# A hybrid mixer network on one core: score blocks, gate products and normaliser sums issued over two and four column groups

## The chip, the cores and the metric

The kernel runs on one core of one Trainium2 chip. The metric is the device time of one execution in microseconds (us), the median of several runs. TensorE (PE in the profile, PEld for its weight loads), VectorE (DVE), ScalarE (ACT), GpSimd (POOL) and the DMA queues run beside each other and meet at semaphores. Everything is float32; each product in the source becomes two matmul instructions with a weight load each.

## The reference

Two streams of 128 tokens (prompt and sample), width 1024, go through four layers. A layer is a mixer and a mixture of 16 experts; the mixers are attention, mLSTM, gated linear attention (GLA), attention. What the change touches:

```
# mLSTM, 8 heads: gates from 32 columns of the input projection
g = (p[..., 2*qk_w + 2*v_w:] + b_gates).reshape(B, T, 2, 2, H)   # direction, gate, head
# state for the last token: the normaliser, per direction and head
n_new = decay * n + einsum('bsh,bshd->bhd', ws, kc)
# GLA: scores inside a chunk, 4 heads x 2 streams, two directions
A = einsum('bcthd,bcshd,bctshd->bchts', qc, kc, exp(diff))       # s <= t
```

The 256 tokens of both streams lie on the free axis of most products, so a product has 256 columns.

## The kernel before, in words

Every engine has its own program, written out by hand; the order of work on an engine is the order of its lines. Weights come in chunks of 2 MB over SyncE's queue (`load`, L462 to L468), in the order of a list (`plan_chunks`, L120). Six ring slots hold them, and three more places in the expert stages. The load of a chunk into a slot waits until TensorE has used the chunk that was there before (`used`, L402); so loads are paced by TensorE's progress.

**mLSTM gates.** POOL fetches the 32 gate columns in four pieces at the start (L532) into `WGT`, which holds for each of 8 slices k of the width two blocks of 40 columns (input gates, forget gates; direction 0 in columns 0 to 7, direction 1 in 32 to 39). TensorE's `mlstm` (L1162 to L1169) multiplies slice by slice: for the first gate, k = 0 to 7 as the slices of the normalised input `H` become ready (`h_ready`, L1025: ScalarE's L618 and VectorE's L1716 write them), then k = 0 to 7 for the second gate. Both go into bank 7 of PSUM. VectorE adds the biases and takes an absolute value (L1794 to L1796, semaphore step `l_abs`). TensorE waits for `l_abs` before the first group of the input projection (L1175), since bank 7 is used later in that stage for modulation rows. ScalarE waits for the same step, applies Exp and Ln (L685, L686), and then copies the projection results out (L695); VectorE continues with scans and the short convolution (L1798 to L1827).

**Input projection.** 16 groups of 8 products (`group`, L962, matmuls at L966), 4 from each chunk, then the rows of two modulation chunks (`mod_rows`, L990 to L997). In `mod_rows` the 8 slices go to four column groups of the array: slice k writes partitions 32*(k%4) to 32*(k%4)+31 of bank 7 with 32-column weights.

**Normaliser.** Within the output projection of mLSTM (L1333 to L1335) eight products, one for each head, add into one result of 8 partitions. The weights of head h are 8 columns cut from a constant with a single column of ones, so that head h lands in row h. ScalarE copies the 8 rows (L809) and stores them with one DMA (L810). Before the next norm ScalarE waits for all small stores (L947).

**GLA.** In `gla` the eight groups i of the gate projection (L1396) alternate with eight blocks of scores (L1399 to L1406). Block i has the 32 query rows of block `blk` of direction d as weights (32 columns) and the keys of one of two buffers `gKI[:, i % 2]` as moving data (128 columns), 8 products for heads and streams. It writes partitions 32*blk to 32*blk+31 of two banks. Before it TensorE waits until the keys are written (`g_ki`, VectorE L1956); VectorE waits for `g_a` before it writes a key buffer again (L1952) and clears both between the directions (L1954). `turn_keys` (L1376) and `state` (L1384) lie between later blocks. ScalarE applies the exponentials of the keys (L847) and copies the groups (L849).

**Expert stages.** Each layer ends with a stage of 8 pairs of experts (L1538, L1549 and others), 96 MB of weights.

Of the kernel before, what the change touches and what calls it, by code (L numbers as in the profile page):

```python
# [17 lines left out]
ALU = mybir.AluOpType  # L18
ACT = mybir.ActivationFunctionType
AX = mybir.AxisListType  # L20

P = 128
# [21 lines left out]
def constants():  # L44
# [35 lines left out]
    add("fold", (i[:, None] % 32 == np.arange(32)[None, :]))  # L80
    add("first", np.broadcast_to(np.tril(np.ones((4, 4)), -1).reshape(1, 16), (P, 16)))
# [69 lines left out]
def plan_slots():  # L151
# [25 lines left out]
    "tensor_step": ["prmT", "a_rotk0", "a_dup0", "l_g", "l_at", "l_kt", "l_n",  # L177
# [3 lines left out]
    "scalar_step": ["cs", "l_rowexp", "l_n_sb", "g_u_sb", "g_se", "g_gate", "g_root0", "g_root1", "y_sq0", "y_sq1", "y_sq2", "y_sq3", "y_root"],  # L181
# [20 lines left out]
def program(nc, I, O):  # L202

    with ExitStack() as ctx:
# [25 lines left out]
        WGT = sb("WGT", [P, KD, 2, 40])  # L230
# [110 lines left out]
        mJ = WGT[:, :, :, :].rearrange("p a b c -> p (a b c)")[:, 0:256]  # L341
# [20 lines left out]
        WA1 = WGT[:, :, :, :].rearrange("p a b c -> p (a b c)")[:, 0:512].rearrange("p (k n) -> p k n", k=KD)  # L362
# [98 lines left out]
        def _(sp):  # L461
# [54 lines left out]
            sp.wait_ge(S("out"), 16 * (4 + 3 + 2 + 2))  # L516
# [7 lines left out]
        def _(pool):  # L524
# [3 lines left out]
            gates = I["mlstm1_w_in"].rearrange("(k p) n -> p k n", p=P)[:, :, 6144:6176]  # L528
            for d in range(2):
                for g in range(2):  # L530
                    at = 16 * d + 8 * g
                    pool.dma_start(WGT[:, :, g, 32 * d:32 * d + 8], gates[:, :, at:at + 8]).then_inc(S("load_g"), 16)  # L532
                    pool.dma_start(BGT[32 * d:32 * d + 8, g:g + 1],
                                   I["mlstm1_b_gates"][at:at + 8].rearrange("(h o) -> h o", o=1)).then_inc(S("load_g"), 16)
                pool.dma_start(M0[32 * d:32 * d + 8, 1:2], I["state_mlstm_m_1"][0, d].rearrange("(h o) -> h o", o=1)).then_inc(S("load_g"), 16)
# [13 lines left out]
            pool.wait_ge(S("out"), 80)  # L549
# [6 lines left out]
            pool.wait_ge(S("out"), 80)  # L556
# [9 lines left out]
        def _(act):  # L566
# [115 lines left out]
            def mlstm():  # L682
                E = mROW[0:40, 2]
                after(act, "l_abs")
# [124 lines left out]
                run(A(mJ[0:8], PS[0:8, 4, 0:N2], ACT.Copy), "l_n_sb")  # L809
                load(O["n"][0].rearrange("d h k -> h d k"), mJ[0:8].rearrange("h (d k) -> h d k", d=2), "out")  # L810
# [129 lines left out]
            for l in range(DEPTH):  # L940
                norm(2 * l)
                if l == 0:
                    mods(0)
                affine(2 * l, l, 0)
                wait(act, "back", 32 * l)
                (lambda: attention(l // 3, l), mlstm, gla)[l % 3]()
                act.wait_ge(S("out"), (32, 80, 112, 144)[l])  # L947
                norm(2 * l + 1)
                affine(2 * l + 1, l, 3)
                moe(l)  # L950
# [8 lines left out]
        def _(pe):  # L959
# [202 lines left out]
            def mlstm():  # L1162
                pe.wait_ge(S("load_g"), 16 * 11)
                for g in range(2):
                    for k in range(KD):
                        if g == 0:
                            h_ready(2, k)
                        ins = mm(PS[0:40, 7, N2 * g:N2 * g + N2], WGT[:, k, g], H[:, k], start=(k == 0), stop=(k == KD - 1))
                ins.then_inc(S("l_g"), 1)  # L1169
                for c in range(4):  # L1170
                    w = landed(pe, POS["min", 1, c])
                    for m in range(4 * c, 4 * c + 4):
                        wait(pe, "l_raw", m - 3)
                        if m == 0:
                            after(pe, "l_abs")  # L1175
                        group(bank(m % 4, 0, N2), zip(tile(w, m % 4), [H[:, k] for k in range(KD)]), "l_qk")
                    mod_run(2, 2 * c, 2 * c + 2)
# [131 lines left out]
                for c in range(2):  # L1309
                    for r in range(2):  # L1310
                        w = landed(pe, POS["mout", 1, (c, r)])
                        for m in range(4):
# [18 lines left out]
                            if c == 1 and r == 1 and m == 0:  # L1331
                                pe.wait_ge(S("l_c_sb"), 5)
                                for h in range(MH):  # L1333
                                    ins = mm(PS[0:8, 4, 0:N2], c_("win")[:, 40 - h:48 - h], mKW[:, h].rearrange("p a b -> p (a b)"), start=(h == 0), stop=(h == MH - 1))
                                ins.then_inc(S("l_n"), 1)  # L1335

            def gla():
# [54 lines left out]
                for i in range(2 * NB):  # L1392
# [81 lines left out]
            def moe(l):  # L1474
                n0 = POS["wg", l, 0]
                n = 2 * l + 1
                if l == 0:
                    pe.wait_ge(S("load_g"), 16 * 11)
# [192 lines left out]
        def _(v):  # L1671
# [117 lines left out]
            def mlstm():  # L1789
# [3 lines left out]
                v.wait_ge(S("load_g"), 16 * 11)  # L1793
                run(ts(gi, PS[0:40, 7, 0:N2], BGT[:, 0:1], None, ALU.add), "dve")  # L1794
                run(ts(gf, PS[0:40, 7, N2:512], BGT[:, 1:2], None, ALU.add), "dve")
# [420 lines left out]
```

## Time and profile before

| | |
|---|---|
| median of 3 runs | 1841.28 us (1840.45 to 1841.54) |
| span of the profiled execution | 1840.1 us |
| own time of the profiled execution | not listed; the median stands 1.2 us above the span |
| TensorE busy | 1752.0 us, 95% |
| DMA read | 606.67 MB, 335 GB/s over the span |
| mLSTM mixer with its gates | about 427 to 764 us |
| GLA mixer | about 1018 to 1191 us |

In the rows a line begins with its start in us and its length. "PE L966 MATMUL ... x64" is a run of 64 matmul instructions of line 966 of the kernel. "[1.68 <-DVE ...]" says that the engine had been idle for 1.68 us, and what ended it.

### The profile page before, as it was taken

To read this page: it belongs to the slowest core of one execution; us is meant where nothing else is said; L and a number is where in the kernel's file an instruction comes from. 1 tells how busy PE (TensorE), PEld (TensorE's weight loads), DVE (VectorE), ACT (ScalarE), POOL (GpSimd) and SP (SyncE) were. 2 spreads that over 40 slices of the span, in tenths; PEclk is the share of its full clock that TensorE was granted. 3 is DMA by queue.
4 is the path that set the end of the run, shared out by engine and by line. 5 is a ranking of instruction groups with operands and counts; after the bars stand their busy time and mean duration, and the time that the engine had idled before them with its cause. 6 is when DMAs were issued, how large, how long until landed. Compare 5 with 4: busy or idle time off the path is not lost.

```text
span 1840.1 us, 21589 instructions
## 1 busy us (share of the span) xinstructions
PE 1752.0 (95%) x8789; PEld 1023.2 (56%) x8789; DVE 475.1 (26%) x1237; ACT 378.3 (21%) x761; POOL 40.6 (2%) x52
## 2 busy tenths in 40 slices
PE   5899999999998979999998999999999999999996
PEld 3578544446744868844444747854444687544433
DVE  2142411115300261321111254251111252511112
ACT  2232200003102480300001233220000342200001
POOL 1000000000000000000000000000000000000000
PEclk9999899999999999999999999999999999899999
DMA  9988699998999235489999795869999819699993
GB/s 343 382 292 372 259 425 425 427 420 293 355 366 316 95 134 206 152 327 427 427 427 410 280 358 207 325 260 420 427 428 421 312 67 387 242 423 426 427 427 145
DMA packets 134526, 609.99 MB, mean 332 GB/s; under 512 B 12485, under 2 KB 19269, under 8 KB 109592
## 3 DMA queue, kind: packets, MB, share of 16 engines
q1 hardware_dynamic: 117408, 589.84, 80.5%
q10 hardware_dynamic: 12504, 10.70, 1.9%
q0 software_dynamic: 4512, 8.02, 1.2%
q8 instruction: 73, 1.20, 0.3%
q14 instruction: 29, 0.24, 0.0%
HBM read 606.67 MB, written 8.92 MB: 335 GB/s over the span
## 4 chain that ended last, share of the span: by engine, by line
PE 82%; DMA 9%; DVE 4%; ACT 2%; issue 1%; SPq 1%; ACTq 0%; DVEq 0%; POOLq 0%
PE PS L966 22%; PE PS L1538 21%; PE PS L1549 11%; PE PS L1502 7%; PE PS L996 4%; DMA ring<-in_moe_wg 3%; PE PS L1049 3%; DMA arena<-in_moe_wu 2%; DMA arena<-token_rows,IDX 2%; DVE arena L2095 1%; DMA ring<-in_attn_w_qkv 1%; PE PS L1017 1%; PE PS L1482 1%; DMA ring<-in_w_mod 1%; PE PS L1543 1%
## 5 line engine op out<-in xcount | busy, mean ns | idle before, releaser
L1538 PE MATMUL PS<-ring,arena 128*64 128x512 f32 x1280 | 375.4, 601 | 4.4 <-DMA ring<-in_moe_wg 4.0
L900 ACT ACTIVATE arena<-PS 128x512 f32<-128x512 f32 (+1 forms) x130 | 70.6, 543 | 803.5 <-PE PS L1529 351.8
L1538 PEld LDWEIGHTS PS<-ring,arena 128*64 128x64 f32 x1280 | 117.0, 138 | 181.6 <-issue 181.6
L2095 DVE TENSOR_TENSOR arena<-arena,PS 128x512 f32<-128x512 f32 x32 | 33.5, 1047 | 641.7 <-PE PS L1538 641.7
L966 PE MATMUL PS<-HS,ring 128*128 128x256 f32 x768 | 175.1, 386 | 4.6 <-ACT arena L735 2.9
L1538 PE MATMUL PS<-arena 128*64 128x512 f32 x576 | 169.6, 594 | 0.0
L966 PEld LDWEIGHTS PS<-HS,ring 128*128 128x128 f32 x768 | 146.0, 193 | 31.0 <-issue 8.3
L966 PE MATMUL PS<-arena,ring 128*128 128x256 f32 x640 | 143.6, 384 | 8.3 <-DVE arena L1893 6.2
L1502 PE MATMUL PS<-arena 128*128 128x256 f32 (+3 forms) x688 | 144.6, 361 | 6.1 <-ACT arena L900 3.7
L1549 PE MATMUL PS<-ring,arena 128*64 128x512 f32 x640 | 141.7, 595 | 0.0
L1502 PEld LDWEIGHTS PS<-arena 128*128 128x128 f32 (+1 forms) x688 | 112.2, 190 | 45.1 <-issue 22.7
L966 PEld LDWEIGHTS PS<-arena,ring 128*128 128x128 f32 x640 | 122.6, 193 | 26.4 <-issue 8.1
L966 PE MATMUL PS<-ring,HS 128*128 128x512 f32 (+1 forms) x256 | 105.0, 568 | 0.0
L1538 PE MATMUL PS<-HS,arena 128*64 128x512 f32 x192 | 92.9, 641 | 0.0
L996 PE MATMUL PS<-ring,CS 128*32 128x512 f32 x768 | 89.8, 606 | 1.9 <-issue 1.3
L1549 PEld LDWEIGHTS PS<-ring,arena 128*64 128x64 f32 x640 | 44.1, 137 | 83.3 <-issue 80.5
L1549 PE MATMUL PS<-arena 128*64 128x512 f32 x192 | 84.9, 595 | 0.1
L1549 PE MATMUL PS<-HS,arena 128*64 128x512 f32 x192 | 85.0, 595 | 0.0
L2076 DVE COPY arena<-PS 128x512 f32<-128x512 f32 (+1 forms) x100 | 68.6, 686 | 52.6 <-PE PS L1543 26.2
L1538 PEld LDWEIGHTS PS<-arena 128*64 128x64 f32 x576 | 52.5, 137 | 53.2 <-issue 53.2
L966 PEld LDWEIGHTS PS<-ring,HS 128*128 128x128 f32 x256 | 48.1, 190 | 56.1 <-issue 55.2
L1049 PE MATMUL PS<-HS,ring 128*128 128x256 f32 x256 | 63.0, 392 | 3.8 <-DMA ring<-in_attn_w_qkv 3.8
(344 smaller groups left out, 1631.9 us busy)
## 6 DMA issues: line engine op xcount, KB each, us to landing
ring<-in_w_mod SPq DMA_DIRECT2D x48, 2048.0 KB, 16.4
ring<-in_moe_wu SPq DMA_DIRECT2D x41, 2048.0 KB, 20.5
ring<-in_moe_wd SPq DMA_DIRECT2D x41, 2048.0 KB, 21.7
ring<-in_moe_wg SPq DMA_DIRECT2D x41, 2048.0 KB, 20.4
arena<-in_moe_wg SPq DMA_DIRECT2D x24, 2048.0 KB, 18.1
HS<-in_moe_wu SPq DMA_DIRECT2D x12, 2048.0 KB, 18.6
arena<-in_moe_wu SPq DMA_DIRECT2D x12, 2048.0 KB, 21.2
arena<-in_moe_wd SPq DMA_DIRECT2D x12, 2048.0 KB, 25.9
```

Source lines behind the costliest of these rows:

```text
L900: A(dst, src, func).then_inc(S(sem), 1)
L966: ins = mm(out, a, b, start=first and i == 0, stop=final and i == len(pairs) - 1)
L996: ins = mm(PS[r:r + 32, 7, :], CS[:, k, 30 - 2 * i:62 - 2 * i], w[:, k], start=(i == 0 and k < 4), stop=(i == len(MODS[g]) - 1 and k >= 4))
L1017: ins = mm(bank(7 if n else 5, 0, N2), ones, SQ[:, k], start=(k == 0), stop=(k == KD - 1))
L1049: ins = mm(bank(5 + m % 2, 0, N2), w[:, k, P * (m % 4):P * (m % 4) + P], H[:, k], start=(k == 0), stop=(k == KD - 1))
L1482: ins = mm(bank(4 + s, 0, NE), H[:, k, T * s:T * s + T], RW[:, k], start=(k == 0), stop=(k == KD - 1))
L1502: return mm(out, rows, onehot, start=first, stop=final, skip_group_check=True)
L1538: ins = mm(PS[64 * e:64 * e + 64, b, :], XG[:, k, 64 * e:64 * e + 64], w[:, k], start=(k == 0), stop=(k == KD - 1))
L1543: ins = tp(bank(b, P * f, P * f + P), HID[:, P * f:P * f + P], ident)
L1549: ins = mm(PS[64 * e:64 * e + 64, b, :], HTS[:, f, 64 * e:64 * e + 64], w[:, f, 512 * j:512 * j + 512], start=(f == 0), stop=(f == 3))
L2076: v.tensor_copy(dst, src).then_inc(S(sem), 1)
L2095: tt(by_k(HID), row(SG), row(bank(here[1])), ALU.mult).then_inc(S("hid"), 1)
```

## The change

It alters three places.

1. **Gates.** `WGT` gets 512 columns; one DMA brings all 32 gate columns, so that slice k has one 32-column weight. Eight products (slice k to column group k%4, bank 6) take the place of sixteen. ScalarE copies bank 6 to `mGP`. Two more products with a constant of 0 and 1 (`foldg`) add the four partial sums and spread them to the 40 rows that VectorE expects, in bank 5. These stand behind group m = 0 of the input projection, and the wait for `l_abs` moves from before group 0 to behind group 3.
2. **Normaliser.** Head h goes to column group h%4, with 32-column weights; heads h and h+4 share a group. ScalarE copies all 128 partitions, and four DMAs of two rows each take the place of one. The counts of the waits for stores follow.
3. **GLA scores.** Blocks i-1 and i are issued together behind group i for odd i, product by product in turn; they write different partitions. `turn_keys(0)` moves from behind block 2 to behind blocks 2 and 3.

```diff
@@ constants
+    foldg = np.zeros((P, 2, 40))
+    for g in range(2):
+        for d in range(2):
+            for h in range(MH):
+                foldg[:, g, 32 * d + h] = (i % 32 == 16 * d + 8 * g + h)
+    add("foldg", foldg.reshape(P, 80))
@@ gpsimd
+            pool.dma_start(mWG, gates).then_inc(S("load_g"), 16)
...
-                    pool.dma_start(WGT[:, :, g, 32 * d:32 * d + 8], gates[:, :, at:at + 8]).then_inc(S("load_g"), 16)
@@ scalar, mlstm
+                after(act, "l_gp")
+                run(A(mGP, bank(6, 0, N2), ACT.Copy), "l_gp_sb")
                 after(act, "l_abs")
...
-                run(A(mJ[0:8], PS[0:8, 4, 0:N2], ACT.Copy), "l_n_sb")
-                load(O["n"][0].rearrange("d h k -> h d k"), mJ[0:8].rearrange("h (d k) -> h d k", d=2), "out")
+                run(A(mJ, bank(4, 0, N2), ACT.Copy), "l_n_sb")
+                for j in range(4):
+                    load(O["n"][0].rearrange("d (r j) k -> j r d k", j=4)[j], mJ[32 * j:32 * j + 2].rearrange("r (d k) -> r d k", d=2), "out")
...
-                act.wait_ge(S("out"), (32, 80, 112, 144)[l])
+                act.wait_ge(S("out"), (32, 128, 160, 192)[l])
@@ tensor, mlstm
-                for g in range(2):
-                    for k in range(KD):
-                        if g == 0:
-                            h_ready(2, k)
-                        ins = mm(PS[0:40, 7, N2 * g:N2 * g + N2], WGT[:, k, g], H[:, k], start=(k == 0), stop=(k == KD - 1))
-                ins.then_inc(S("l_g"), 1)
+                for k in range(KD):
+                    h_ready(2, k)
+                    r = 32 * (k % 4)
+                    ins = mm(PS[r:r + 32, 6, 0:N2], mWG[:, k], H[:, k], start=(k < 4), stop=(k >= 4))
+                ins.then_inc(S("l_gp"), 1)
+
+                def gates():
+
+                    after(pe, "l_gp_sb")
+                    for g in range(2):
+                        ins = mm(PS[0:40, 5, N2 * g:N2 * g + N2], c_("foldg")[:, 40 * g:40 * g + 40], mGP, start=True, stop=True)
+                    ins.then_inc(S("l_g"), 1)
+
...
                         wait(pe, "l_raw", m - 3)
+                        group(bank(m % 4, 0, N2), zip(tile(w, m % 4), [H[:, k] for k in range(KD)]), "l_qk")
                         if m == 0:
+                            gates()
+                        if m == 3:
                             after(pe, "l_abs")
-                        group(bank(m % 4, 0, N2), zip(tile(w, m % 4), [H[:, k] for k in range(KD)]), "l_qk")
...
-                                    ins = mm(PS[0:8, 4, 0:N2], c_("win")[:, 40 - h:48 - h], mKW[:, h].rearrange("p a b -> p (a b)"), start=(h == 0), stop=(h == MH - 1))
+                                    ins = mm(PS[32 * (h % 4):32 * (h % 4) + 32, 4, 0:N2], c_("win")[:, 40 - h // 4:72 - h // 4], mKW[:, h].rearrange("p a b -> p (a b)"), start=(h < 4), stop=(h >= 4))
@@ tensor, gla
-                    d, blk, lo, hi = gla_block(i)
-                    pe.wait_ge(S("g_v_sb"), 4)
-                    pe.wait_ge(S("g_ki"), i + 1)
-                    pe.wait_ge(S("g_qi"), d + 1)
-                    for hs in range(8):
-                        ins = mm(PS[GB * blk:GB * blk + GB, 2 * d + hs // 4, T * (hs % 4):T * (hs % 4) + T],
-                                 gQI[:, d, hs, GB * blk:GB * blk + GB], gKI[:, i % 2, hs], start=True, stop=True)
-                    ins.then_inc(S("g_a"), 1)
-                    if i == 2:
+                    if i % 2:
+                        d = i // NB
+                        pe.wait_ge(S("g_v_sb"), 4)
+                        pe.wait_ge(S("g_ki"), i + 1)
+                        pe.wait_ge(S("g_qi"), d + 1)
+                        for hs in range(8):
+                            for j in (i - 1, i):
+                                blk = gla_block(j)[1]
+                                ins = mm(PS[GB * blk:GB * blk + GB, 2 * d + hs // 4, T * (hs % 4):T * (hs % 4) + T],
+                                         gQI[:, d, hs, GB * blk:GB * blk + GB], gKI[:, j % 2, hs], start=True, stop=True)
+                                if hs == 7:
+                                    ins.then_inc(S("g_a"), 1)
+                    if i == 3:
                         turn_keys(0)
```

VectorE reads the gates from bank 5 in place of bank 7. The waits on `load_g` count 8 DMAs in place of 11.

## Rows read from the trace of the kernel before

**Rows 1.** The page: span, TensorE, and the chain that ended last by engine.

```profile
span 1840.1 us, 21589 instructions
...
PE 82%; DMA 9%; DVE 4%; ACT 2%; issue 1%; SPq 1%; ACTq 0%; DVEq 0%; POOLq 0%
```

**Rows 2.** Windows: length, busy time and count by engine; then PEclk, DMA share, GB/s.

```profile
750.00:760.00 10.00, 10.00 (x47) 8.84 (x47) 1.22 (x4) 3.49 (x9) 0.00 (x0) 1.00 0.02 5
770.00:780.00 10.00, 9.83 (x51) 9.10 (x50) 5.81 (x27) 7.13 (x10) 0.00 (x0) 0.66 0.27 81
820.00:830.00 10.00, 10.00 (x48) 4.55 (x46) 0.00 (x0) 0.60 (x1) 0.00 (x0) 1.00 1.01 434
...
1130.00:1140.00 10.00, 10.00 (x63) 8.56 (x63) 3.05 (x4) 3.26 (x5) 0.00 (x0) 1.00 0.13 47
```

**Rows 3.** Waits of SyncE's queue, 740 to 1180 us: total, times, longest.

```profile
SPq L468 <- PE PS L966: 153.8, 9, 23.6
```

**Rows 4.** The timeline of all engines around the gates.

```profile
426.86 4.35 ACT L618 ACTIVATE HS<-HS,MC 128x128 f32<-128x128 f32 x8 [2.43 <-DVE HS L1704]
...
427.48 8.03 PE L1168 MATMUL PS<-HS,WGT 128*40 128x256 f32 x32 [0.17 <-ACT HS L618]
...
437.14 1.28 ACT L685 ACT_TABLE_LOAD   x1 [5.93 <-DVE HS L1796]
...
437.19 14.05 PE L966 MATMUL PS<-HS,ring 128*128 128x256 f32 x64 [1.68 <-DVE HS L1796]
...
440.98 0.38 ACT L695 ACTIVATE HS<-PS 128x256 f32<-128x256 f32 x1 [0.40 <-PE PS L966]
...
448.26 0.35 DVE L1825 TENSOR_SCALAR arena<-HS,prm 128x256 f32<-128x256 f32 x1
```

**Rows 5.** The chain of work in the GLA stage: start, length, what.

```profile
1098.77 1.86 PE PS L1404 x16
1100.64 3.65 PE PS L966 x16
...
1111.67 0.59 PE PS L1381 x4
1112.25 3.46 PE PS L966 x16
...
1119.28 1.75 PE PS L1404 x16
```

**Rows 6.** The timeline: matmuls over four and over two column groups.

```profile
451.17 3.64 PE L996 MATMUL PS<-ring,CS 128*32 128x512 f32 x32
...
77.22 1.95 PE L1108 MATMUL PS<-arena,consts 128*64 128x256 f32 x16
```

**Rows 7.** The chain of work at the normaliser.

```profile
746.51 3.55 PE PS L1334 x16
```

**Rows 8.** The timeline of ScalarE behind the normaliser.

```profile
750.50 0.32 ACTq L571 DMA_DIRECT2D out_n<-WGT  x1
...
752.16 2.71 ACT L609 ACTIVATE HS<-X 128x256 f32<-128x256 f32 x6
...
757.91 0.42 ACT L609 ACTIVATE HS<-X 128x256 f32<-128x256 f32 x1 [3.04 <-DVE X L1724]
```

**Rows 9.** Line 1404's weight loads: ns (min/median/max), first and last start.

```profile
L1404 PEld LDWEIGHTS PS<-arena x128: 106/110/110, 1098.7 to 1144.8; 128*32 128x32 f32 x128
```

**Rows 10.** The timeline of VectorE's key writes in GLA.

```profile
1100.89 0.69 DVE L1956 TENSOR_TENSOR arena<-arena 128x512 f32<-128x512 f32 x1
...
1121.59 1.76 DVE L1954 MEMSET arena<- 128x2048 f32 x1 [8.14 <-PE PS L1404]
...
1127.02 0.69 DVE L1956 TENSOR_TENSOR arena<-arena 128x512 f32<-128x512 f32 x1
```

**Rows 11.** DMA issues: KB each, median us from issue to landing.

```profile
consts<-in_consts ACTq DMA_DIRECT2D x1, 757.5 KB, 6.4
...
WGT<-in_mlstm_w_in POOLq DMA_DIRECT2D x4, 32.0 KB, 6.5
```

More of the change, by code:

```diff
@@ L176 @@
 STEPS = {
-    "tensor_step": ["prmT", "a_rotk0", "a_dup0", "l_g", "l_at", "l_kt", "l_n",
+    "tensor_step": ["prmT", "a_rotk0", "a_dup0", "l_gp", "l_g", "l_at", "l_kt", "l_n",
                     "g_u", "g_at0", "g_at1", "a_rotk3", "a_dup3"],
@@ L180 @@
                     "a_ropek3", "y_sum"],
-    "scalar_step": ["cs", "l_rowexp", "l_n_sb", "g_u_sb", "g_se", "g_gate", "g_root0", "g_root1", "y_sq0", "y_sq1", "y_sq2", "y_sq3", "y_root"],
+    "scalar_step": ["cs", "l_gp_sb", "l_rowexp", "l_n_sb", "g_u_sb", "g_se", "g_gate", "g_root0", "g_root1", "y_sq0", "y_sq1", "y_sq2", "y_sq3", "y_root"],
 }
@@ L229, in program @@
         SK = sb("SK", [P, 2, HEADS])
-        WGT = sb("WGT", [P, KD, 2, 40])
+        WGT = sb("WGT", [P, 512])
         BGT = sb("BGT", [40, 2])
@@ L340, in program @@
         mCO = [RS[:, :, :].rearrange("p a b -> p (a b)").rearrange("p (j d k) -> p j d k", j=2, d=2), sm(0, 2, 2, T)]
-        mJ = WGT[:, :, :, :].rearrange("p a b c -> p (a b c)")[:, 0:256]
+        mJ = WGT[:, 0:256]
+        mWG = WGT[:, 0:256].rearrange("p (k n) -> p k n", k=KD)
+        mGP = sq(768, N2)
         gQ, gK = ar(0, 8, T), ar(1024, 8, T)
@@ L361, in program @@
         gSS, gRT, gRN = sm(0, 2, GH), sm(8, 2, GH), sm(16, 2, GH)
-        WA1 = WGT[:, :, :, :].rearrange("p a b c -> p (a b c)")[:, 0:512].rearrange("p (k n) -> p k n", k=KD)
+        WA1 = WGT[:, 0:512].rearrange("p (k n) -> p k n", k=KD)
         WA2 = ar(16896, 512)[0:64]
@@ L515, in _ @@
                 sp.dma_start(O[y][0], XR[:, s]).then_inc(S("out"), 16)
-            sp.wait_ge(S("out"), 16 * (4 + 3 + 2 + 2))
+            sp.wait_ge(S("out"), 16 * (4 + 6 + 2 + 2))
             for j in range(2):
@@ L548, in _ @@
             pool.wait_ge(S("x"), KD * 4)
-            pool.wait_ge(S("out"), 80)
+            pool.wait_ge(S("out"), 128)
             pool.memset(WA1, 0.0).then_inc(S("pad"), 1)
@@ L555, in _ @@
             pool.wait_ge(S("x"), KD * 5)
-            pool.wait_ge(S("out"), 80)
+            pool.wait_ge(S("out"), 128)
             for d in range(2):
@@ L1162, in mlstm @@
             def mlstm():
-                pe.wait_ge(S("load_g"), 16 * 11)
-                for g in range(2):
-                    for k in range(KD):
-                        if g == 0:
-                            h_ready(2, k)
-                        ins = mm(PS[0:40, 7, N2 * g:N2 * g + N2], WGT[:, k, g], H[:, k], start=(k == 0), stop=(k == KD - 1))
-                ins.then_inc(S("l_g"), 1)
+                pe.wait_ge(S("load_g"), 16 * 8)
+                for k in range(KD):
[8 more added lines that the diff above has]
+                    ins.then_inc(S("l_g"), 1)
                 for c in range(4):
@@ L1477, in moe @@
                 if l == 0:
-                    pe.wait_ge(S("load_g"), 16 * 11)
+                    pe.wait_ge(S("load_g"), 16 * 8)
                 for k in range(KD):
@@ L1792, in mlstm @@
                 after(v, "l_g")
-                v.wait_ge(S("load_g"), 16 * 11)
-                run(ts(gi, PS[0:40, 7, 0:N2], BGT[:, 0:1], None, ALU.add), "dve")
-                run(ts(gf, PS[0:40, 7, N2:512], BGT[:, 1:2], None, ALU.add), "dve")
+                v.wait_ge(S("load_g"), 16 * 8)
+                run(ts(gi, PS[0:40, 5, 0:N2], BGT[:, 0:1], None, ALU.add), "dve")
+                run(ts(gf, PS[0:40, 5, N2:512], BGT[:, 1:2], None, ALU.add), "dve")
                 run(stt(e, gf, -1.0, gf, ALU.mult, ALU.max), "l_abs")
```

## The prediction

> **What bounds the kernel now.** I read the page first: the span is 1840.1 us and the chain that ended last runs through TensorE for 82% and through DMA for 9% [rows 1]. So I ask of each place that the change touches whether TensorE is what the others wait for there, and then whether the stage behind it is bound by loads that would not start earlier. The windows answer the second. In the expert stage the DMA engines are full (share 1.01, 434 GB/s at 820 to 830 us), but just before it they are almost idle (0.02 at 750 to 760 us), and likewise in the middle of GLA (0.13 at 1130 to 1140 us) [rows 2]. No backlog of loads is carried over these points. The waits of SyncE's queue say why: from 740 to 1180 us it stood 153.8 us behind matmuls of L966 alone [rows 3]. Loads are started by TensorE's progress. If TensorE reaches the end of mLSTM or GLA earlier, the full stretch behind starts earlier by the same, and ends earlier by the same. I therefore add up TensorE's time in three places and pass it on whole.
>
> **Gates.** Now: 32 matmuls from 427.48 us, 8.03 us long, the first 16 paced by ScalarE, which hands out eight slices until 426.86 + 4.35 = 431.21 us. Then VectorE works, and the projection starts at 437.19, after an idle 1.68 us [rows 4]. One matmul of 256 columns takes 3.46 / 16 = 0.216 us in a stream [rows 5]. After: the eight products still follow the slices. The last slice comes at 431.2; with 0.1 us for the semaphore and 2 x 0.216 its product ends at 431.75, and with 0.1 us of changeover the projection starts at 431.85. It is 5.35 us earlier. Added: two fold products, 4 x 0.216 = 0.86 us, and the change of the weights' shape and back. That changeover I take from GLA, where the group behind a score block lasts 3.65 and one behind full-width work 3.46 [rows 5]: 0.2 us, and 0.1 on entry. Net gain 5.35 - 1.15 = 4.2 us.
>
> What is hidden: ScalarE's added copy (0.38 us, as L695 [rows 4]) runs under group 0 of 3.46 us. The folds end near 436.5, so `l_abs` comes near 438.5, about 1.4 us later than now (437.14 [rows 4]), and all of ScalarE's and VectorE's chain with it. Behind ScalarE's wait stands the first copy of the projection (440.98 now [rows 4], about 442.4 then); who needs it is group 4, at 431.85 + 4 x 3.46 + 1.15 + 3.64 for the modulation rows [rows 6] = 450.5. That is 8 us of cover. The first convolution step (448.26 now) comes near 449.8, and the copy of group 4, at about 454, is the first to need it. The wait for `l_abs` behind group 3 (at 446.8) is long met. Cost nothing; if the cover were gone, at most the 1.4 us.
>
> **Normaliser.** Now 3.55 us for 16 matmuls [rows 7]. After, the same 16 over four column groups. The trace has four groups only with 512 columns: 32 matmuls in 3.64 us [rows 6], so 16 of half the length take about 0.91. Gain 3.55 - 0.91 = 2.6 us. Bounds: 0 if groups did not overlap at 256 columns, 2.7 at most. I take 2.6, since two groups at just this 256 columns ran 16 matmuls in 1.95 us with the last one's tail [rows 6], twice as fast as one.
>
> Three more stores: ScalarE's queue takes 0.32 us for one [rows 8], so the last of four goes out 1.0 us later, on a start 2.6 us earlier. The norm behind waits for their landing. Now it has six squares done at 752.16 + 2.71 = 754.87 and then stands still until 757.91 for its input [rows 8]. Three us of slack cover 1.0 us more. Cost nothing; without that slack nothing either, as the start is earlier by more.
>
> **GLA scores.** Now each of eight blocks costs 1.86 us and 0.19 us more in the group behind it (3.65 against 3.46) [rows 5]: 2.05, together 16.4. One matmul of the block takes (1.86 - 0.11) / 16 = 0.109. After: four pairs of 32 matmuls. If the two column groups run side by side, a pair takes 16 steps of 0.109 and the same changeover, 2.05; four make 8.2, gain 8.2 us. If they do not, a pair takes 32 x 0.109 + 0.11 + 0.19 = 3.8, four 15.2, gain 1.2. I take the first. Its nearest rows are the two-group one at 256 columns [rows 6] and the form itself [rows 9]: a weight load lasts 0.110 us, so it just fits behind a matmul step of 0.109, as it does today, and the other group has its own.
>
> A rule speaks against it. By the Trainium skill (TensorE: Matmul & The Clock Gate, Part 3: Packing small matmuls) a weight load overlaps matmuls in flight only when the row group differs, and here all use all rows. Taken literally, load and step would stand one behind the other. Today's block already contradicts it: 16 loads of 0.110 and 16 steps of 0.109 lie within 1.86 us, not 3.5 [rows 5, 9].
>
> The waits. Pairing brings later blocks' keys nearer. Where block 0 began (1098.77), group 1 now follows, and the pair starts at 1098.77 + 3.46 = 1102.2 [rows 5]. Its second keys are written by 1100.89 + 0.69 = 1101.58 [rows 10]. Slack 0.6. The clearing of the key buffers waits for block 3. Now that block ends at 1119.28 + 1.75 = 1121.03, the clearing begins at 1121.59 and the sixth keys are done at 1127.02 + 0.69 = 1127.71, 6.7 behind the block [rows 5, 10]. In the new order block 3 ends at 1102.2 + 1.86 + 3.65 + 3.46 + 3.64 + 1.86 = 1116.7, the sixth keys are there at 1123.4, and TensorE wants them after the turned keys and two groups, at 1116.7 + 0.59 + 2 x 3.46 = 1124.2. Slack 0.8; the eighth keys, by the same kind of count, have some 0.6. So cost nothing, but it is thin: up to 0.5 to 1 us a pair if a handover is slower. The moved `turn_keys(0)` is wanted only by a copy that stands behind the clearing.
>
> **Start.** POOL issues one gate load for four [rows 11], and nobody waits for it. The constants grow by 80 columns, 40 KB; that share of 6.4 us [rows 11] is 0.3 at worst, against fewer small pieces. I take 0, bounds -0.3 to +0.3.
>
> **Sum.** 4.2 + 2.6 + 8.2 = 15.0 us. Against the profiled 1840.1 that gives 1825.1; the median stands 1.2 above that span, so 1841.3 - 15.0 = 1826.3.
>
> The granted clock adds scatter. At 770 to 780 us it is 0.66 of full [rows 2]: 6.8 us at the lower level of 1.2 GHz, a price of 3.4 us, after TensorE had stood waiting behind the norm and at the router. When work shifts, one or two such stretches may come or go, each half of that, about 1.7 us.
>
> **The rivals.**
> (a) Column groups do not overlap at 128 columns. Gain 1.2 instead of 8.2: 1833.3. For: no row has two groups so short. Against: [rows 6]. Chance 5%.
> (b) The DMA-bound end of an expert stage swallows what mLSTM gains (6.8): 1833.1; if what GLA gains too, 1841. For: the full DMA share. Against: the idle windows before it [rows 2]. 4% and 3%.
> (c) Slower. The array holds back the weight load of one column group while the other streams. Then each matmul of a pair costs 0.110 + 0.109 = 0.219, a pair 32 x 0.219 + 0.3 = 7.3 in place of 4.1, four +12.8. The normaliser costs 16 x (0.110 + 0.216) = 5.2, +1.7; the gates keep -4.2, since the pace of the slices covers it. Sum +10.3: 1851.6. With the other two gains whole it turns the sign once a pair takes over (16.4 + 6.8) / 4 = 5.8 us. Against: [rows 6]. Chance 3%. The skill's rule above, read literally, is this mechanism.
> (d) The thin slacks in GLA turn into waits, four of 0.5 to 1 us: 1828.3 to 1830.3, within the range. 10%. The forecast as such has 75%.
>
> **How the numbers follow.** 1826.3 is the sum. Below it the range has two clock stretches and the 0.3 of the start, 1822.5; above, waits in GLA and a clock stretch, 1831.0. It leaves out (a), (b) and (c), 15%, and little of the forecast's own. A measurement of this kernel can tell 0.2%, 3.7 us, from no change. Faster by more than that: the forecast, (a), the first half of (b), and (d): 94%. Within: 3%. Slower: 3%.
>
> **What would show it.** The profile after should have 16 gate matmuls and the projection starting near 431.9; the normaliser's 16 in 0.9 us; four runs of 32 score matmuls of about 1.9 us; `l_abs` near 438.5; no wait of TensorE for L1956; expert stages of unchanged length. Score runs of 3.6 us would show (a), of 7 us (c); a longer DMA wait at the end of the expert stages (b).

## The result, and the profile after

| | before | after |
|---|---|---|
| median of the runs, us | 1841.12 (1840.45 to 1841.54, 4 runs) | 1821.82 (1818.57 to 1823.27, 4 runs) |
| ratio, 95% interval | | 0.9895 (0.9881 to 0.9909) |
| span of the profiled execution, us | 1840.1 | 1816.7 |

The kernel is 19.3 us faster. The forecast was 15.0 us, 1826.3, with a range down to 1822.5; the median lies 0.7 us below that. The profiled execution after is the fastest of its four (1818.57), so I use it for the length of stages, and the medians for the whole.

The page of the kernel after, against [rows 1]: the chain still runs through TensorE.

```profile
span 1816.7 us, 21563 instructions
...
PE 84%; DMA 8%; DVE 4%; ACT 2%; issue 1%; SPq 0%; ACTq 0%; DVEq 0%; POOLq 0%
```

**Gates.** The timeline of the kernel after, against [rows 4]; L1178 holds the products over four column groups, L1185 the folds, L1818 to L1820 VectorE's part that ends with `l_abs`.

```profile
423.42 4.41 PE L1178 MATMUL PS<-HS,WGT 128*32 128x256 f32 x16 [0.17 <-ACT HS L626]
...
427.76 3.72 PE L977 MATMUL PS<-HS,ring 128*128 128x256 f32 x16
427.95 0.38 ACT L693 ACTIVATE HS<-PS 128x256 f32<-128x256 f32 x1 [0.79 <-PE PS L1178]
...
431.41 1.06 PE L1185 MATMUL PS<-HS,consts 128*40 128x256 f32 x4
...
433.58 0.42 DVE L1820 SCALAR_TENSOR_TENSOR HS<-HS 40x256 f32<-40x256 f32 x1
...
446.52 5.66 PE L977 MATMUL PS<-HS,ring 128*128 128x256 f32 x25
```

The last line there is the start of the second chunk's groups. In the kernel before it was:

```profile
454.75 5.45 PE L966 MATMUL PS<-HS,ring 128*128 128x256 f32 x24
```

From the first gate product to the projection it was 437.19 - 427.48 = 9.71 us and is 427.76 - 423.42 = 4.34: a gain of 5.37 where 5.35 was forecast. The folds and the shape changes give back about 1.2, so the second chunk's groups start 446.52 - 423.42 = 23.10 us behind the first product instead of 454.75 - 427.48 = 27.27: 4.17 us nearer (4.2 forecast). The projection has no idle time ahead of it.

**Normaliser.** The chain of the kernel after from the normaliser (L1354) to the first expert matmuls (L1562), against [rows 7].

```profile
736.31 1.00 PE PS L1354 x16
737.31 10.56 PE PS L977 x48
...
758.50 1.04 PE PS L1506 x8
759.54 3.28 PE PS L1511 x16
...
770.44 4.87 PE PS L1562 x21
```

The same chain of the kernel before.

```profile
750.06 10.56 PE PS L966 x48
...
770.07 3.44 PE PS L1482 x16
773.51 3.49 PE PS L1487 x16
...
784.52 5.72 PE PS L1538 x25
```

The 16 normaliser matmuls take 1.00 us where they took 3.55. The whole stretch from them to the experts takes 770.44 - 736.31 = 34.13 us instead of 784.52 - 746.51 = 38.01. So 3.88 us went, 1.3 more than the normaliser's own 2.55, all of it in the norm and router (L1482 to L1487 before, L1506 to L1511 after). These two windows, with the columns of [rows 2], tell why: the kernel before first, then the kernel after.

```profile
767.00:777.00 10.00, 9.82 (x52) 9.17 (x51) 7.14 (x27) 7.75 (x13) 0.00 (x0) 0.66 0.11 32
```

```profile
754.00:764.00 10.00, 9.81 (x58) 8.78 (x57) 7.71 (x30) 8.70 (x14) 0.00 (x0) 0.83 0.19 62
```

A mean granted clock of 0.66 of the 2.4 GHz level is 6.8 us at 1.2 GHz, 0.83 is 3.4 us.

**GLA scores.** The chain of the kernel after, against [rows 5]: L1427 are the pairs.

```profile
1078.37 7.10 PE PS L977 x32
1085.47 1.87 PE PS L1427 x32
1087.34 7.10 PE PS L977 x32
...
1098.02 1.75 PE PS L1427 x32
1099.76 0.59 PE PS L1401 x4
1100.35 6.91 PE PS L977 x32
1107.26 1.87 PE PS L1427 x32
...
1118.35 1.76 PE PS L1427 x30
...
1138.48 27.86 PE PS L977 x128
```

The first group and the output projection in the chain of the kernel before:

```profile
1095.12 3.65 PE PS L966 x16
...
1163.46 27.86 PE PS L966 x128
```

A pair of 32 matmuls takes what a block of 16 took, 1.87 us, and the changeover is paid once in two groups (7.10 for 32 against 2 x 3.46 = 6.92). The chain shows no wait between them, so the thin slacks in the keys held. From the first group to the output projection it is 1138.48 - 1078.37 = 60.11 us instead of 1163.46 - 1095.12 = 68.34: 8.23 us went.

**Start.** The DMA engines in the first 30 us: their busy tenths and GB/s in 40 slices of 0.75 us, and what they moved. Before:

```profile
DMA  0077999999999999999989999999999999999999
GB/s 0 0 82 177 394 373 416 368 394 284 258 207 256 368 302 185 339 178 372 271 298 331 377 388 385 390 377 390 391 391 385 385 385 382 393 388 385 388 385 388
DMA packets 5373, 9.60 MB, mean 320 GB/s; under 512 B 944, under 2 KB 1312, under 8 KB 5373
```

After:

```profile
DMA  0056999999999999999999999999999999999999
GB/s 0 0 63 188 343 382 413 436 360 348 314 357 362 333 390 232 336 407 393 292 380 393 396 390 385 390 380 391 388 388 382 388 393 382 385 390 388 382 390 385
DMA packets 5600, 10.27 MB, mean 342 GB/s; under 512 B 896, under 2 KB 1264, under 8 KB 5600
```

The engines are as busy in both, but from 7 to 15 us they move less in the kernel before: 0.67 MB by the end, which is 1.7 us at the 385 GB/s of the last slices. TensorE waits for those loads. Its first matmuls on the second chunk of the attention weights, in the timeline before and then after:

```profile
69.49 5.41 PE L1049 MATMUL PS<-HS,ring 128*128 128x256 f32 x16 [3.77 <-DMA ring<-in_attn_w_qkv]
```

```profile
67.13 3.72 PE L1060 MATMUL PS<-HS,ring 128*128 128x256 f32 x16 [2.31 <-DMA ring<-in_attn_w_qkv]
```

They start 2.36 us earlier. The 16 of them also take 3.72 instead of 5.41 us, since in the profiled execution before a stretch of 3.4 us at 1.2 GHz fell on them, and after it fell on L1007's matmuls at 32 to 36 us, before a wait for loads. By the start of the mLSTM gates the two differ by 427.48 - 423.42 = 4.06 us: 2.4 of loads and 1.7 of clock.

So the three TensorE terms are 4.17 + 2.55 + 8.23 = 14.95 us, as forecast (15.0). What is over lies at the start and in the granted clock.

### The profile page after: what moved, and what is told of

Read it like the earlier page. It is cut to its first block, busy times and chain, and to the rows that moved or that the text cites. A ratio compares the mean times of both kernels' runs of the same rounds, so it can differ in the third digit from the quotient of the medians.

```text
span 1816.7 us, 21563 instructions
## 1 busy us (share of the span) xinstructions
PE 1734.2 (95%) x8777; PEld 1010.1 (56%) x8777; DVE 475.3 (26%) x1237; ACT 378.7 (21%) x762; POOL 37.9 (2%) x49
## 3 DMA queue, kind: packets, MB, share of 16 engines
q0 software_dynamic: 4432, 8.02, 1.2%
## 4 chain that ended last, share of the span: by engine, by line
PE 84%; DMA 8%; DVE 4%; ACT 2%; issue 1%; SPq 0%; ACTq 0%; DVEq 0%; POOLq 0%
PE PS L1562 22%; PE PS L977 22%; PE PS L1573 11%; PE PS L1526 7%; PE PS L1007 4%; DMA ring<-in_moe_wg 3%; PE PS L1060 3%; DMA arena<-in_moe_wu 2%; DVE arena L2119 2%; PE PS L1028 1%; DMA ring<-in_attn_w_qkv 1%; PE PS L1506 1%; DMA ring<-in_w_mod 1%; PE PS L1567 1%; PE PS L1548 1%
## 5 line engine op out<-in xcount | busy, mean ns | idle before, releaser
L1562 PE MATMUL PS<-ring,arena 128*64 128x512 f32 x1280 | 376.0, 601 | 2.4 <-DMA ring<-in_moe_wg 2.2
L1562 PEld LDWEIGHTS PS<-ring,arena 128*64 128x64 f32 x1280 | 117.2, 138 | 179.5 <-issue 179.5
L977 PE MATMUL PS<-HS,ring 128*128 128x256 f32 x768 | 172.9, 383 | 2.9 <-ACT arena L745 2.9
L1562 PE MATMUL PS<-arena 128*64 128x512 f32 x576 | 169.6, 594 | 0.0
L1526 PEld LDWEIGHTS PS<-arena 128*128 128x128 f32 (+1 forms) x688 | 112.2, 190 | 44.1 <-issue 22.7
L1562 PE MATMUL PS<-HS,arena 128*64 128x512 f32 x192 | 93.5, 644 | 0.0
L1007 PE MATMUL PS<-ring,CS 128*32 128x512 f32 x768 | 89.2, 603 | 3.8 <-DMA ring<-in_w_mod 2.3
L1562 PEld LDWEIGHTS PS<-arena 128*64 128x64 f32 x576 | 52.5, 137 | 53.2 <-issue 53.2
L1060 PE MATMUL PS<-HS,ring 128*128 128x256 f32 x256 | 61.3, 384 | 2.3 <-DMA ring<-in_attn_w_qkv 2.3
## 6 DMA issues: line engine op xcount, KB each, us to landing
ring<-in_moe_wu SPq DMA_DIRECT2D x41, 2048.0 KB, 20.4
```

The lines of the kernel that those rows point to most:

```text
L977: ins = mm(out, a, b, start=first and i == 0, stop=final and i == len(pairs) - 1)
L1007: ins = mm(PS[r:r + 32, 7, :], CS[:, k, 30 - 2 * i:62 - 2 * i], w[:, k], start=(i == 0 and k < 4), stop=(i == len(MODS[g]) - 1 and k >= 4))
L1060: ins = mm(bank(5 + m % 2, 0, N2), w[:, k, P * (m % 4):P * (m % 4) + P], H[:, k], start=(k == 0), stop=(k == KD - 1))
L1526: return mm(out, rows, onehot, start=first, stop=final, skip_group_check=True)
L1562: ins = mm(PS[64 * e:64 * e + 64, b, :], XG[:, k, 64 * e:64 * e + 64], w[:, k], start=(k == 0), stop=(k == KD - 1))
```

## The experiments

Theory S: the start gains as well, because one load in 1024 rows of 128 bytes costs the DMA engines less than four with 4096 rows of 32 bytes, and TensorE waits for what stands behind. Rival K: the start gives nothing, the excess is scatter of the stretches of lower clock. Each kernel is held against runs of the kernel before from the same group and chip, with medians of 1839.34 us (17 runs; for e_load4, e_load8, e_defer, b_defer), 1841.36 (17; a_again, b_start, e_gla_seq, e_gla_old), 1839.89 (17; e_gates_only, e_gates_start, e_norm_old, b_gla) and 1839.45 (10; e_load16, a_third). The last two groups ran on one chip. The times are medians with their extent and count.

### Undoing or moving the start

`e_load4` and `e_load8`: the kernel after, its gate columns in four pieces (shown) or eight.

```diff
-            pool.dma_start(mWG, gates).then_inc(S("load_g"), 16)
+            for j in range(4):
+                pool.dma_start(mWG[:, :, 8 * j:8 * j + 8], gates[:, :, 8 * j:8 * j + 8]).then_inc(S("load_g"), 16)
```

> The changed kernel with the gate columns fetched in four pieces of 8 columns again (rows of 32 bytes, as before the change) in place of one of 32 columns (rows of 128 bytes). Theory (small pieces rob the DMA engines in the first 15 us, when all engines are busy and the first weights are waited for): the start is slower again, the second weight slot lands near 22.9 us in place of 21.4, the GB/s of 6 to 15 us fall back from about 345 to about 285, and the time rises by 1.5 to 2.4 us plus clock scatter, to 1823.5 to 1826. Rival (the constants or mere scatter of the clock made the start faster): landings and time as in the changed kernel, 1820 to 1823.

> The same with eight pieces of 4 columns (rows of 16 bytes): twice the small rows of four pieces. Theory that the number of small rows sets the cost: 8192 rows against 4096 and 1024, so the second slot lands about 2 us later than with four pieces (near 25 us), and the time is 2 us above four pieces, 1825 to 1829. Rival (bytes, not rows, or scatter): as with one piece.

`e_defer` and `b_defer`: the kernel after, and the one before, with POOL's start loads put off.

```diff
+            pool.wait_ge(S("a_q"), 8)
             gates = I["mlstm1_w_in"].rearrange("(k p) n -> p k n", p=P)[:, :, 6144:6176]
```

> The changed kernel, with POOL's start loads (gate columns, gate biases, initial maxima, router weights) put off until attention has worked on its first heads, near 90 us. Nobody needs them before 175 us. Theory: the remaining 1024 rows of the gates, 1024 of the router and the biases leave the crowded first 15 us, and the start gains another 0.5 to 1.5 us: 1819.5 to 1821.5. Rival (the small rows do not matter): no change, or a little slower if they then meet the loads of attention.

> The kernel before, with POOL's start loads put off in the same way. Theory: all small rows leave the start, so this alone gives what the single load gave and more: 2.5 to 4 us faster than the kernel before, 1837 to 1838.5, with the second slot landing at 21 us or earlier. Rival (scatter of the clock explained the start): within 1 us of the kernel before.

`b_start`: the kernel before, with the one load, and four copies by GpSimd into the padded layout.

```diff
-                    pool.dma_start(WGT[:, :, g, 32 * d:32 * d + 8], gates[:, :, at:at + 8]).then_inc(S("load_g"), 16)
+            WGL = sm(320, KD, 32)
+            pool.dma_start(WGL, gates).then_inc(S("load_a"), 16)
...
+                    pool.tensor_copy(WGT[:, :, g, 32 * d:32 * d + 8], WGL[:, :, at:at + 8]).then_inc(S("pad"), 1)
```

> The kernel before, with the start of the change alone: one load of the gate columns in rows of 128 bytes instead of four loads in rows of 32 bytes, and four small copies by GpSimd into the padded layout, which nothing waits for. Theory S: the second landing in ring slots 1 and 3 comes 1.3 to 2.3 us earlier than in the kernel before, and the whole is 1.5 to 2.5 us faster (ratio about 0.9989). Rival K: the landings stay within 0.3 us, and so does the time, apart from the scatter of the clock stretches.

`a_again`: the kernel after itself.

> The changed kernel unaltered, beside the kernel before and three others on one chip, so that all are held against the same runs. The three TensorE terms of the sum are 14.8 us by the trace (4.2 + 2.5 + 8.1). Theory S (the start gains as well, some 2.2 us, since 1024 rows of 128 bytes take the place of 4096 of 32): about 17 us off the kernel before, scatter of the clock stretches +-2 us on top. Rival K (the start gives nothing and the rest of the 19.3 us was scatter of the clock stretches): about 15 us off.

Measured. The third column is the start of the attention matmuls shown above, the fourth what the DMA engines moved in the first 30 us.

| kernel | time, us | matmuls, us | MB |
|---|---|---|---|
| before (profiled) | | 69.49 | 9.60 |
| after (profiled) | 1821.82 | 67.13 | 10.27 |
| a_again | 1818.65 (1817.40 to 1820.41, 4) | 67.13 | 10.27 |
| e_load4 | 1819.83 (1817.07 to 1820.63, 5) | 68.99 | 9.57 |
| e_load8 | 1824.41 (1817.89 to 1826.31, 6) | 71.42 | 8.68 |
| e_defer | 1821.74 (1815.85 to 1822.35, 6) | 66.65 | 10.50 |
| b_defer | 1835.59 (1831.65 to 1839.07, 12) | 67.20 | 10.45 |
| b_start | 1839.79 (1836.02 to 1846.28, 12) | 67.68 | 10.25 |

The last two columns follow the pieces of the gate load, whatever else the kernel has. With one piece the matmuls start at 67.0 to 67.7 us in eight traces (mean 67.25), with four at 69.0 to 69.5 in four (mean 69.31), with eight at 71.4. Where the loads are put off the start is 66.65 and 67.20, although b_defer still has four pieces. That part is shown. The whole times are blurred. The ratios to the kernel before are 0.9882 (0.9859 to 0.9905) for a_again, 0.9891 (0.9873 to 0.9909) for e_load4, 0.9918 (0.9901 to 0.9934) for e_load8, 0.9976 (0.9962 to 0.9990) for b_defer and 0.9991 (0.9976 to 1.0005) for b_start. The last, 1.6 us in the median, is of the size that S gives, but its interval holds K too, and four pieces cost nothing that shows: e_load4's interval and a_again's overlap almost whole. b_defer is 3.8 us faster than the kernel before, and its interval (1.8 to 7.0 us) leaves out K's "within 1 us". Several expectations were missed in the whole time: e_load4 (1819.83, 1823.5 at least expected), e_load8 and e_defer by less than 1 us, b_defer (1835.59, 1837 expected at least), and a_again, which was 22.7 us faster than its base where S had 17 and 2 of scatter.

### The disputed cost made five times as large

`e_load16`: as e_load4 with 16 pieces of two columns, 16384 rows of 8 bytes; `a_third` is the kernel after beside it.

> The changed kernel with its gate columns loaded in 16 pieces, 16384 rows of 8 bytes, a cost well above the scatter. From one, four and eight pieces the landings in ring slot 3 came at 32.1, 33.9 and 36.0 us, about 0.53 us a piece; so 16 pieces should land there near 40.2. Theory S (what the start costs in landings is passed on whole): the execution is about 8 us slower than the changed kernel beside it. Rival K (the expert stages or the clock take it in): less than 4 us slower, and the projection of mLSTM starts less than 4 us later.

> The changed kernel unaltered, as the base for e_load16 on the same chip. Against the kernel before: the terms as now measured are gates 4.2, normaliser with the clock behind it 3.9, GLA 8.1, start 1.8 to 2.4, together 18.0 to 18.6; theory: within 2 us of that. If it were 15.0, the start and the clock behind the normaliser would not be in it.

e_load16 took 1828.88 us (1823.36 to 1835.15, 6 runs), a_third 1819.30 (1817.13 to 1821.20, 5 runs; ratio to before 0.9888, 0.9872 to 0.9905). That is 9.6 us for the 15 added pieces, 15360 rows where the change took away 3072. a_third stood 20.2 us below its base, at the upper end of what was expected. The timeline of e_load16 has both ends of it:

```profile
76.25 3.72 PE L1061 MATMUL PS<-HS,ring 128*128 128x256 f32 x16 [2.69 <-DMA ring<-in_attn_w_qkv]
...
432.20 4.41 PE L1179 MATMUL PS<-HS,WGT 128*32 128x256 f32 x16 [0.17 <-ACT HS L627]
```

The timeline of a_third:

```profile
67.42 5.41 PE L1060 MATMUL PS<-HS,ring 128*128 128x256 f32 x16 [3.28 <-DMA ring<-in_attn_w_qkv]
...
425.45 4.41 PE L1178 MATMUL PS<-HS,WGT 128*32 128x256 f32 x16 [0.17 <-ACT HS L626]
```

The attention matmuls start 76.25 - 67.42 = 8.8 us later than in a_third. The gate products start 6.75 us later; a_third had lost 1.7 us to the lower clock on the attention matmuls (5.41 instead of 3.72), which makes it 8.4. Against a_again (423.45), which had no such stretch there, it is 8.8. What the start costs is passed on whole or nearly so, in the rows and in the time. Rival K falls. The price is linear in the pieces: 8.8 / 15 = 0.59 us for each one more, that is for 1024 more rows, at the same 128 KB. The DMA engines of e_load16 in the first 30 us:

```profile
DMA  0057999999999999999999999999999999999999
GB/s 1 0 66 208 349 382 396 404 358 268 218 148 230 175 194 192 149 154 135 163 186 208 242 154 144 150 162 156 179 221 235 354 364 373 391 380 385 385 380 219
DMA packets 4331, 7.09 MB, mean 236 GB/s; under 512 B 941, under 2 KB 1565, under 8 KB 4331
```

From 3 us on they are at nine tenths or more, and yet move 135 to 242 GB/s between 8 and 22 us. By that price the 3072 rows that the change takes away are worth 1.8 us; pairs of the kernels above show 1.8 to 2.4 (b_start and the kernel before, a_again and e_load4, e_gates_start and e_gates_only, the kernels after and before), and the two means differ by 2.1. I take 2.1.

Where does the time go? The queues of the kernel after in the same 30 us, q1 with SyncE's loads, q10 with ScalarE's and q0 with GpSimd's (packets, MB, share of the 16 engines' time), and then those of e_load16:

```profile
q1 hardware_dynamic: 3952, 8.00, 75.1%
q10 hardware_dynamic: 1376, 2.08, 19.8%
q0 software_dynamic: 272, 0.20, 2.5%
```

```profile
q1 hardware_dynamic: 2414, 4.88, 63.4%
q10 hardware_dynamic: 1376, 2.08, 33.3%
q0 software_dynamic: 540, 0.13, 6.6%
```

GpSimd's queue, which has the gates, takes 4.1% more, 1.2 us of 30. The same 1376 packets of ScalarE's queue take 13.5% more, 4.1 us, and SyncE's gets through 2414 packets in 63.4% of the time where it got through 3952 in 75.1%. So most of the loss is booked on the loads that share the engines: their packets last longer. The trace doesn't resolve the rows: over the whole execution GpSimd's queue lists 464 packets more than in the kernel after (4896, 4432), for 15360 more rows. And in every one of these kernels each piece of the gates brings 1024 rows, so a price for a row can't be told from a price for a DMA. Pieces that keep rows of 128 bytes would tell them apart; none was run.

### Does the alternation matter, or only the pairing?

`e_gla_seq`: the kernel after, the 16 matmuls of a pair's first block issued before the 16 of its second.

```diff
-                        for hs in range(8):
-                            for j in (i - 1, i):
-                                blk = gla_block(j)[1]
+                        for j in (i - 1, i):
+                            blk = gla_block(j)[1]
+                            for hs in range(8):
```

> The changed kernel; each pair of score blocks is still issued behind one wait, but the 16 matmuls of the first block come before the 16 of the second, rather than one of each in turn. Theory (two column groups run beside each other only when their matmuls are neighbours in the stream): a pair takes 2 x 1.75 + 0.1 = 3.6 us instead of 1.87, four pairs +6.9 us, as the loss of most of the 8.1 us. Rival (what helps is the pairing: one wait and one changeover instead of two): a pair stays at 1.9 us and the time within 0.5 us.

The chain of e_gla_seq, to be read against the one of the kernel after:

```profile
1084.07 3.20 PE PS L1427 x32
1087.28 7.10 PE PS L977 x32
...
1097.95 3.08 PE PS L1427 x32
...
1101.62 6.91 PE PS L977 x32
1108.53 3.20 PE PS L1427 x32
```

A pair takes 3.20 us instead of 1.87, four pairs 5.3 us more; I had expected 3.6 and 6.9. Most of the overlap is between neighbours in the stream. From the last modulation rows before the first group to the output projection GLA takes 71.91 us in the kernel before, 69.02 in e_gla_seq and 63.68 in the kernel after: pairing alone brings 2.9 of the 8.2 us, alternation the other 5.3. The whole took 1821.59 us (1820.13 to 1823.27, 4 runs), 2.9 more than a_again; at 1290 us the profiled executions stood 5.3 us further apart than they had before the first group, and by the end the spans differed by 2.6 only. Other stretches of lower clock are the likely reason.

Rival (c) of the prediction rested on weight loads. The loads of the kernel after:

```profile
L1427 PEld LDWEIGHTS PS<-arena x128: 106/110/110, 1085.4 to 1119.8; 128*32 128x32 f32 x128
```

32 loads of 0.110 us, 3.5 us in all, lie within the 1.87 us of a pair together with 32 matmuls. So loads of one column group run beside matmuls, and beside loads, of the other, though all use all rows. The rule of the Trainium skill that the prediction weighed (TensorE: Matmul & The Clock Gate, Part 3) does not hold for these groups in its literal reading.

### The parts alone

`e_gla_old` is the kernel after with the score blocks one by one; `b_gla` is the kernel before with the pairs alone.

```diff
-                    if i % 2:
-                        d = i // NB
+                    d, blk, lo, hi = gla_block(i)
...
-                    if i == 3:
+                    if i == 2:
                         turn_keys(0)
```

> The changed kernel with GLA's score blocks one by one as before, the rest kept. If the parts add up as the milestones of the trace say, GLA's eight groups and blocks take 8.1 us more and the whole is 8.1 us slower than the changed kernel on this chip; if the loads behind GLA swallowed part of it, the matmul rows show 8.1 and the whole less than 6.

> The kernel before with the pairs of GLA score blocks alone. The term measured by the trace is 8.1 us; undoing it in the changed kernel cost 10.0 us by medians. Theory: 8.1 us faster, the rest being scatter of the clock stretches. Rival (pairing also takes a stretch of lower clock away, the one at 1012 or at 1204 us): about 10 us faster.

e_gla_old took 1828.69 us (1825.87 to 1830.55, 6 runs), 10.0 more than a_again. In the two profiled executions, the spans differ by 8.3. b_gla took 1832.21 us (1826.69 to 1839.32, 8 runs), 7.7 less than the kernel before; its ratio is 0.9964 (0.9944 to 0.9984). Both are in keeping with 8.2. Nothing of GLA's gain is swallowed by the loads behind it (rival b).

`e_norm_old` is the kernel after with the old normaliser.

```diff
-                                    ins = mm(PS[32 * (h % 4):32 * (h % 4) + 32, 4, 0:N2], c_("win")[:, 40 - h // 4:72 - h // 4], mKW[:, h].rearrange("p a b -> p (a b)"), start=(h < 4), stop=(h >= 4))
+                                    ins = mm(PS[0:8, 4, 0:N2], c_("win")[:, 40 - h:48 - h], mKW[:, h].rearrange("p a b -> p (a b)"), start=(h == 0), stop=(h == MH - 1))
...
-                for j in range(4):
-                    load(O["n"][0].rearrange("d (r j) k -> j r d k", j=4)[j], mJ[32 * j:32 * j + 2].rearrange("r (d k) -> r d k", d=2), "out")
+                load(O["n"][0].rearrange("d h k -> h d k"), mJ[0:8].rearrange("h (d k) -> h d k", d=2), "out")
```

`e_gates_start` is e_norm_old with e_gla_old's blocks, so that gates and start are left; `e_gates_only` also has e_load4's four pieces, so that the gates are left.

> The changed kernel with the normaliser in one column group and its one store, as before. By the matmul rows alone 2.5 us slower than the changed kernel. Theory N: TensorE's wait behind mLSTM and the stretch of lower clock that follows it (6.8 us in each trace of a kernel with the old normaliser, 3.4 us in each trace with the new one) belong together, so the stretch at about 765 us is 6.8 us long again and the whole 2.5 + 1.7 = 4.2 us slower. Rival: the stretch stays 3.4 us long and the whole is 2.5 us slower.

> As e_gates_only, but with the one load in 128-byte rows. Theory S: landings at the start 1.5 to 2.3 us earlier than in e_gates_only, and 1 to 2.3 us less in all, so 5.5 to 6.5 us off the kernel before. Rival K: the start gives nothing, 4.2 us.

> The change's gates alone: GLA's score blocks one by one and the normaliser in one column group as before, and the gate columns loaded in four pieces of 32-byte rows, so that the start is as before too. The forecast's term is 4.2 us off the kernel before. A rival (the gates give more than the milestones say, by the stretches of lower clock behind them) would give 6 us or more.

| kernel | time, us | ratio to before, 95% | normaliser to experts, us |
|---|---|---|---|
| e_norm_old | 1825.04 (1818.37 to 1825.60, 6) | 0.9909 (0.9887 to 0.9932) | 776.15 - 738.14 = 38.01 |
| e_gates_start | 1828.64 (1827.03 to 1831.30, 6) | 0.9935 (0.9914 to 0.9955) | 773.23 - 736.55 = 36.68 |
| e_gates_only | 1833.08 (1827.51 to 1838.44, 10) | 0.9961 (0.9945 to 0.9978) | 775.10 - 738.42 = 36.68 |

The last column is the chain shown for the kernels before (38.01) and after (34.13). By the ratios e_norm_old gains 3.9 to 5 us less than a_third and a_again, with the scatter of the whole times on that. In its trace the router is at the lower clock as long as in the kernel before:

```profile
759.00:769.00 10.00, 9.82 (x52) 9.37 (x52) 7.08 (x28) 7.71 (x14) 0.00 (x0) 0.66 0.06 17
```

Alone that would carry theory N. But e_gates_start and e_gates_only have the old normaliser too, and their stretch was 3.4 us long. So N falls as I stated it: the two are not tied. The three lengths separate the terms instead: 38.01 - 36.68 = 1.33 us is the clock, with the same normaliser, and 36.68 - 34.13 = 2.55 is the normaliser, at the same clock. But the edit is not shown to be without effect on it either. It was 3.4 us in all eight traces kept of kernels with the new normaliser and 6.8 us in five of the seven with the old one, which is hardly chance. Why it is so often long there is open.

e_gates_only is 6.8 us faster than the kernel before, e_gates_start 11.3. The interval of the first (4.0 to 10.1) just holds the 4.2 of the forecast. That of the second (8.3 to 15.8) lies above the 6.3 of gates and start. Its six runs had a mean granted clock of 0.980 where those of the kernel before had 0.978, which is worth 3 us of 1840 if counted whole and closes the gap to within 2. e_gates_only's was 0.979, worth 2 us, which leaves 4.6 of its 6.8. The step between the two kernels, 4.4 us, has the sign of S and is larger than the 2.1 us of its rows (matmuls at 67.13 and 69.27).

## Why the prediction was wrong by a little

**Gates: right.** 4.2 forecast, 4.17 in the rows. The last slice paced the products, the copy and VectorE's work were hidden, the folds cost what was taken. `l_abs` is there at 433.58 + 0.42 = 434.0, 6.2 us behind the start of the projection; the forecast had 438.5 - 431.85 = 6.65. Nobody waited for it.

**Normaliser: right.** 2.6 forecast, 2.55 in the rows, and once more between e_gates_start and the kernel after. The 16 matmuls take 1.00 us, where 0.91 was taken. The three more stores cost nothing: the stretch behind is not longer.

**GLA: right.** 8.2 forecast, 8.23 in the rows; undone alone and done alone it was worth 10.0 and 7.7 us. Rivals (a), (b), (c) and (d) all fall: a pair lasts 1.87 us, not 3.6 or 7, the gain reaches the end, and no handover became a wait.

**Start: the step that failed.** The prediction said of it "nobody waits for it" and "I take 0, bounds -0.3 to +0.3". Nobody waits for the gate columns, that is so. But their 4096 rows stood in the same DMA engines as the constants, the input and the attention weights, and TensorE does wait for those. The edit was priced by its bytes (40 KB more constants) and by whose semaphore it is, not by what it does to the loads beside it. [rows 11] had the four loads of 32 KB, and the length of their rows stands in the diff. It measured 1.8 to 2.4 us in the rows; the 2.1 taken is seven times the bound.

**The clock: seen, and taken at nothing in the sum.** The prediction gave 1.7 us for a stretch that comes or goes, either way, and put two of them into the lower end of its range. Over all runs of these kernels (61 of the kernel before, beside the four groups of experiments, and 13 of the kernel after) the mean granted clock was 0.9779 and 0.9788. With (1 - clock) x span of each run, that is 40.7 and 38.5 us below full speed: 2.2 us in favour of the kernel after, with a standard error of 0.8. In those runs the means are 1840.1 and 1819.8, a gain of 20.4 +- 0.7. Terms and clock make 14.95 + 2.1 + 2.2 = 19.3. The remaining 1.1 us I can't assign. The 2.2 may be too much: over the 61 runs of the kernel before, the time rises by 0.72 us for each us so counted. At that rate the clock gave 1.6 us, and 1.7 are left. Whether the change caused this gain of clock is not shown; up to about 1 us of it may be the stretch behind the normaliser (1.33 us, in five traces of seven against none of eight).

The result was 4.3 us beyond the forecast's gain of 15.0. Of these the start is shown, some 2 us; the clock is counted, not shown, for about 2; the rest is open. The sum of the three TensorE terms was right by its mechanism. That the median lies only 0.7 us outside the range is also due to the two clock stretches put into its lower end. Had the start been bounded by its worth, the sum would have been 17.1 and the median forecast 1824.2, with 1821.8 well inside a range of the same width.

## What to carry to other kernels

Where the DMA engines are full and TensorE waits for a load, price every other transfer in that stretch by its count of pieces and contiguous rows, whoever waits for it: here 0.59 us for each further piece with 1024 rows of 32 bytes or less, where the bytes of all of them together, 128 KB, would take 0.34 us at 385 GB/s. Which of the two counts, pieces or rows, stays open. Small products that use few output rows can go side by side over column groups: here 32 took the 1.87 us of 16 over two groups, and 16 took 1.00 instead of 3.55 us over four. Alternate the groups between neighbours in the instruction stream, as without it the 32 took 3.20 us. Where a kernel's time scatters by stretches of the granted clock, judge an edit of 2 us by its rows, or make it several times as large, as the whole times of single edits here disagreed by as much as the edit was worth.

## What the runs showed that I had not expected

- 16 pieces instead of one, of the same 128 KB, cost 9.6 us of 1819, with the DMA engines' busy share at 0.98 in the first 30 us of a_third and 1.03 in those of e_load16. A high busy share does not say that bytes move.
- In e_gla_seq a pair took 3.20 us, less than two blocks alone (2 x 1.75). Some matmuls overlap even without alternation, perhaps at the seam of the two blocks; no row shows where.
- The stretch of 1.2 GHz at the router behind mLSTM was 3.4 us long or its double in every trace looked at, and that moved the time by 1.3 us: 38.01 against 36.68 us for the same instructions.
